# Rotary halves in chunks of their own, scores of 32 rows in fours, the norm's factor in the sine and cosine tables, and the short convolution's product from PSUM

## What is computed

```python
h = rmsnorm(x, mix_norm_g[l])
a_b, a_c, a_x, q, k, v, c_in = split(h @ w_in)            # 256,256,256,512,512,512,512 columns
y_a = a_b * causal_depthwise_conv(a_c * a_x, short_conv_w)  # 3 taps
q = apply_rope(q.reshape(b, s, 2, 4, 64), cos, sin)       # 2 maps x 4 heads of 64
k = apply_rope(k.reshape(b, s, 2, 4, 64), cos, sin)
# apply_rope: x1, x2 = halves of 32;  [x1*cos - x2*sin, x2*cos + x1*sin]
p = softmax(mask(q @ k.T / 8)); a = p[map 0] - lam * p[map 1]; y_b = rmsnorm(a @ v) * (1 - lam_init)
y_c = silu(layernorm(conv31(glu(c_in)) + bias))           # 31 taps: the "filter"
x = x + concat(y_a, y_b, y_c) @ w_out
```

## Time and profile before

| | |
|---|---|
| runs, us | 2670.54, 2681.98, 2677.64 |
| median, us | 2677.64 |
| profiled execution: time / span, us | 2680.19 / 2678.9 |
| mean granted TensorE clock | 0.983 |
| busy: PE, PEld | 2562.9 us (96%), 2112.5 us (79%) |
| busy: DVE, ACT, POOL | 1103.3 us (41%), 945.4 us (35%), 1211.0 us (45%) |

### The profile page before, as it was taken

How to read it: one execution, slowest core, us unless ns; L and a number is a source line. 1 busy time by engine, 2 the same in 40 slices (tenths; PEclk the granted TensorE clock), 3 DMA queues, 4 the chain that set the end, 5 groups by cost and what they waited for, 6 DMA issues and landing times.

```text
span 2678.9 us, 32969 instructions
## 1 busy us (share of the span) xinstructions
PE 2562.9 (96%) x12952; PEld 2112.5 (79%) x12952; DVE 1103.3 (41%) x2303; ACT 945.4 (35%) x1437; POOL 1211.0 (45%) x1597
## 2 busy tenths in 40 slices
PE   6999999999999999998999999999999999999998
PEld 5777888887777888886778788877777787888886
DVE  7965111126964211137656764423345523311112
ACT  4553322234453222244433233324453433322221
POOL 5114665653125656554332332344323554565653
PEclk8999999999999999999999999999998999999998
DMA  4442223225432222232110111122222231223222
GB/s 156 124 111 79 94 81 103 102 83 151 126 95 79 101 92 99 96 108 94 50 48 32 48 37 44 48 95 86 87 79 89 100 110 64 95 92 105 94 89 76
DMA packets 41371, 237.32 MB, mean 89 GB/s; under 512 B 4736, under 2 KB 5888, under 8 KB 18560
## 3 DMA queue, kind: packets, MB, share of 16 engines
q1 hardware_dynamic: 38912, 218.43, 23.4%
q0 software_dynamic: 2304, 16.78, 3.1%
HBM read 214.22 MB, written 4.19 MB: 82 GB/s over the span
## 4 chain that ended last, share of the span: by engine, by line
PE 84%; DVE 10%; ACT 3%; POOL 2%; issue 1%; DMA 0%; SPq 0%; DVEq 0%; ACTq 0%
PE PB L1757 67%; PE PB L1795 4%; PE PB L1759 4%; DVE cc L2413 2%; POOL WL L2788 2%; ACT WH L2016 1%; PE PB L1952 1%; PE PB L1971 1%; PE PB L1769 1%; PE PB L1777 1%; PE PB L1959 1%; PE PB L1919 1%; PE PB L1983 1%; PE PB L1999 1%; PE PB L1940 0%
## 5 line engine op out<-in xcount | busy, mean ns | idle before, releaser
L2788 POOL TENSOR_TENSOR WL<-WR,WH 128x256 fp32r<-128x256 f32 (+1 forms) x1444 | 1041.9, 757 | 789.1 <-ACT WH L2016 789.1
L1757 PE MATMUL PB<-HH,WH 128*128 128x512 f32 x1992 | 803.8, 404 | 12.2 <-ACT HH L2031 10.0
L1757 PE MATMUL PB<-HL,WH 128*128 128x512 f32 x1992 | 783.5, 393 | 1.9 <-DVE HL L2309 1.9
L1757 PE MATMUL PB<-HH,WL 128*128 128x512 f32 x1992 | 520.3, 397 | 2.6 <-POOL WL L2788 2.6
L2016 ACT ACTIVATE WH<-WR 128x2048 fp32r<-128x2048 f32 (+1 forms) x209 | 371.5, 1778 | 260.9 <-PE PB L1757 254.2
L1757 PEld LDWEIGHTS PB<-HH,WH 128*128 128x128 f32 x1992 | 378.4, 190 | 102.8 <-issue 14.3
L1757 PEld LDWEIGHTS PB<-HL,WH 128*128 128x128 f32 x1992 | 378.3, 190 | 80.0 <-issue 3.6
L1757 PEld LDWEIGHTS PB<-HH,WL 128*128 128x128 f32 x1992 | 366.0, 189 | 76.6 <-issue 3.9
L1757 PE MATMUL PB<-BL,WH 128*128 128x512 f32 x848 | 334.1, 394 | 0.8 <-DVE BL L2318 0.8
L1757 PE MATMUL PB<-BH,WH 128*128 128x512 f32 x784 | 310.6, 396 | 2.7 <-ACT BH L2045 2.7
L1757 PE MATMUL PB<-BH,WL 128*128 128x512 f32 x784 | 197.6, 396 | 5.4 <-POOL WL L2788 5.4
(11 more groups left out here) (344 smaller groups left out, 3103.1 us busy)
## 6 DMA issues: line engine op xcount, KB each, us to landing
WR<-in_w_gu SPq DMA_DIRECT2D x66, 1024.0 KB, 4.8
WR<-in_w_dn SPq DMA_DIRECT2D x48, 704.0 KB, 4.1
WR<-in_w_in SPq DMA_DIRECT2D x22, 1024.0 KB, 4.9
WL<-WR POOLq DMA_DIRECT2D x16, 1024.0 KB, 7.0
WR<-in_qkv SPq DMA_DIRECT2D x12, 1024.0 KB, 4.8
WR<-in_w_out SPq DMA_DIRECT2D x8, 1024.0 KB, 4.8
WR<-in_qk SPq DMA_DIRECT2D x8, 1024.0 KB, 4.8
WR<-in_gb SPq DMA_DIRECT2D x4, 1024.0 KB, 4.8
```

Of the source, the lines that this page charges most:

```text
L1757: ins = pe.matmul(out[:, 0:n], wt[:, k * cols + j * P:k * cols + (j + 1) * P], x[:, k, 0:n], start=first, stop=last)
L2788: ins = g.tensor_tensor(m.WL[u % 2][:, part], m.WR[u % 2][:, part], f32(m.WH[u % 2][:, part]), ALU.subtract)
```

## The change

- The weights of q and k are rearranged when the high part is cast: within a unit, the first halves (32 columns) of four heads come first, then their last halves. ScalarE does this in two instructions of 1024 elements, GpSimd reads the raw weights in the same order. So chunk p of `Q` and `K` holds first halves and chunk p + 2 last halves, and the rotation needs no swap of rows. These units (`of_heads`: 2, 3, 5 and 6) always have their low parts from GpSimd; `by_dma` now names units 4 and 7 to 10 in both layers. Before it named 4 to 10 in layer 0 and 2 to 10 in layer 1.
- `qkin` moves to ScalarE and only copies (q times 1/8). There are four buffers `qr`. `rotc` stays on GpSimd; VectorE multiplies `qr` by the sine in place (`rots`), and once both chunks of a pair are there, subtracts one and adds the other (`rot`). The matmul L1819 and its constant go.
- New tables `RCOS` and `RSIN`, `COS` and `SIN` times the norm's factor, are made once a layer on VectorE (`scaled`). The sign of the sine goes.
- `score` makes each product in two matmuls of 32 rows that add up in a bank: four heads' first halves side by side, then their last halves. It waits for all four banks first.
- `short_conv` multiplies the first tile by the square of the factor (`R2`, from ScalarE) and then by the second tile straight from PSUM: one VectorE operation less for each of its two halves.
- The model costs are new for these steps and for some that had none, and `FILTER_LEAD` is 1.0.

The core of the diff (the rest: constants' places, step and semaphore tables, model costs, the same steps' names):

```diff
@@ -137,15 +136,17 @@
     m.POSF, m.ANG, m.KF = run(tail1, end, ("POSF", [P, S]), ("ANG", [P, S]), ("KF", [P, S]))
+    qr2, qr3 = at("qr2", [P, S], b0 + 10 * S * 4)[0], at("qr3", [P, S], b1 + 10 * S * 4)[0]
     m.COS, m.SIN = run(g0, b0, ("COS", [P, S]), ("SIN", [P, S]))
...
     names = [("qr0", [P, S]), ("qr1", [P, S]), ("Q", [P, 4, S]), ("K", [P, 4, S]), ("VT", [P, 4, S]), ("cx", [P, 2 + S]),
-             ("cp0", [P, 30 + S]), ("cp1", [P, 30 + S]), ("cc0", [P, S]), ("cc1", [P, S]), ("ct", [P, S]), ("sm", [P, 96])]
+             ("cp0", [P, 30 + S]), ("cp1", [P, 30 + S]), ("cc0", [P, S]), ("cc1", [P, S]), ("ct", [P, S]), ("sm", [P, 96]), ("rcos", [P, S])]
     names += [(f"pa{i}{n}", [P, S]) for i in range(3) for n in range(2)]
-    m.qr0, m.qr1, m.Q, m.K, m.VT, m.cx, cp0, cp1, cc0, cc1, m.ct, m.sm, *pa = run(g1, b0, *names)
+    m.qr0, m.qr1, m.Q, m.K, m.VT, m.cx, cp0, cp1, cc0, cc1, m.ct, m.sm, rcos, *pa = run(g1, b0, *names)
     pa += run(tail1, end, ("pa30", [P, S]), ("pa31", [P, S]))
-    m.qr, m.cp, m.cc, m.cacc = (m.qr0, m.qr1), (cp0, cp1), (cc0, cc1), m.qr0
+    m.RCOS, m.RSIN, m.R2 = rcos, m.ct, rcos
+    m.qr, m.cp, m.cc, m.cacc = (m.qr0, m.qr1, qr2, qr3), (cp0, cp1), (cc0, cc1), m.qr0
     m.pa = [pa[2 * i:2 * i + 2] for i in range(4)]
@@ -305,8 +306,14 @@
+
+def of_heads(unit):
+    return unit[0] in ("w_in0", "w_in1") and unit[1] in (2, 3, 5, 6)
+
+
+
 def by_dma(unit):
-    return unit[0] in ("w_in0", "w_in1") and unit[1] >= (4 if unit[0] == "w_in0" else 2)
+    return unit[0] in ("w_in0", "w_in1") and unit[1] >= 4 and not of_heads(unit)
@@ -805,7 +812,7 @@
         w = f"w_in{l}"
-        qrs = Ring([Room(0), Room(1)], clock)
+        qrs = Ring([Room(i) for i in range(4)], clock)
         for q in qrs.rooms:
@@ -831,7 +838,8 @@
             step("rope_tab")
-            rope.extend([at("rt4"), at("rt5")])
+            rope.append(at("rt4"))
+        step("scaled", l, rope=rope, r=r, after=f + ct_after[0])
@@ -858,13 +866,14 @@
-        def rotate(name, c, q):
-            room = fbank.take()
-            t = Tile(room, room.after)
-            pe("rot", l, name, c, tile=t, q=q.i, tok=at("qkin", l, name, c), rope=rope, after=f)
-            room.free(at("rots", l, name, c))
-            q.free(at("rot", l, name, c))
-            turned[name, c] = True
+        def turn(name, c, q):
+            step("rots", l, name, c, q=q.i, tok=at("rotc", l, name, c))
+            turned[name, c] = q
+            if c >= 2:
+                first, second = turned[name, c - 2], q
+                step("rot", l, name, c - 2, first=first.i, second=second.i, tok=at("rots", l, name, c))
+                first.free(at("rot", l, name, c - 2))
+                second.free(at("rot", l, name, c - 2))
@@ -875,11 +884,12 @@
                     q = qrs.take()
-                    step("qkin", l, name, c, tile=t, q=q.i, r=r, after=q.after)
+                    step("qkin", l, name, c, tile=t, q=q.i, after=q.after + rope)
+                    step("rotc", l, name, c, q=q.i, tok=at("qkin", l, name, c), after=f)
                     room.free(at("qkin", l, name, c))
                     if waiting:
-                        rotate(*waiting)
-                    waiting = (name, c, q)
+                        turn(*waiting)
+                    waiting = name, c, q
                     yield
@@ -900,22 +910,22 @@
             it = chunks()
-            acc_after = [at("rot", l, "k", 1), at("rot", l, "k", 3)]
+            acc_after = [at("rot", l, "k", 1)]
+            step("r2", l, r=r, after=[at("rotc", l, "k", 1), at("rotc", l, "k", 3)])
             for j in range(2):
                 room, t = yield from tiles_of(it)
-                step("sh1", l, j, tile=t, r=r, after=f)
+                step("sh1", l, j, tile=t, after=f)
                 room.free(at("sh1", l, j))
...
                 room, t = yield from tiles_of(it)
-                step("sh2", l, j, tile=t, after=ct_after[0])
-                room.free(at("sh2a", l, j))
+                step("sh2", l, j, tile=t)
+                room.free(at("sh2", l, j))
                 yield
...
                 room, t = yield from tiles_of(it)
-                step("sh4", l, j, tile=t)
+                step("sh4", l, j, tile=t, after=acc_after)
                 room.free(at("sh4a", l, j))
-                ct_after[0] = [at("sh4", l, j)]
                 step("opv", "mix", l, j, src=m.cacc[:], c=j, tok=at("sh4", l, j), after=b_after)
@@ -1813,23 +1823,20 @@
             pe.matmul(PB[w["tile"].b][:], ones, m.cc[1][:], start=False, stop=True).then_inc(tile, 1)
-        elif kind == "rot":
-            te.all(w["tile"].after)
-            te.wait_ge(*at("qkin", *key))
-            pe.matmul(PB[w["tile"].b][:], m.CON[:, C_SWAP:C_SWAP + P], m.qr[w["q"]][:], start=True, stop=True).then_inc(tile, 1)
         elif kind == "score":
...
             n = P * (qb + 1)
-            for i in range(2):
-                c = 2 * i + pair
-                for k in range(2):
-                    te.all(w["tiles"][2 * i + k].after)
-                te.wait_ge(*at("rot", l, "q", c))
-                te.wait_ge(*at("rot", l, "k", c))
-                for k in range(2):
-                    rows = slice(64 * k, 64 * k + 64)
-                    pe.matmul(PB[w["tiles"][2 * i + k].b][:, 0:n], m.Q[rows, c, qb * P:(qb + 1) * P], m.K[rows, c, 0:n],
-                              start=True, stop=True).then_inc(tile, 1)
+            te.wait_ge(*at("rot", l, "q", pair))
+            te.wait_ge(*at("rot", l, "k", pair))
+            for t in w["tiles"]:
+                te.all(t.after)
+            for half, c in enumerate((pair, pair + 2)):
+                for u in range(4):
+                    rows = slice(32 * u, 32 * u + 32)
+                    ins = pe.matmul(PB[w["tiles"][u].b][:, 0:n], m.Q[rows, c, qb * P:(qb + 1) * P], m.K[rows, c, 0:n],
+                                    start=(half == 0), stop=(half == 1))
+                    if half:
+                        ins.then_inc(tile, 1)
         elif kind == "strans":
@@ -2013,7 +2020,13 @@
                 ae.wait_ge(*o.unit_end[u - 2].done)
-            a.activation(m.WH[u % 2][:, 0:n], m.WR[u % 2][:, 0:n], ACT.Copy).then_inc(sems["whi"], 1)
+            if of_heads(o.units[u]):
+                for j in range(2):
+                    ins = a.activation(m.WH[u % 2][:].rearrange("p (k j h x) -> p j k h x", j=2, h=4, x=32)[:, j],
+                                       m.WR[u % 2][:].rearrange("p (k h j x) -> p j k h x", j=2, h=4, x=32)[:, j], ACT.Copy)
+            else:
+                ins = a.activation(m.WH[u % 2][:, 0:n], m.WR[u % 2][:, 0:n], ACT.Copy)
+            ins.then_inc(sems["whi"], 1)
             if kind == "splitd":
@@ -2076,6 +2089,15 @@
             a.activation(m.cc[j][:], m.cc[j][:], ACT.Silu, bias=vec(f"ln_b{l}", j), scale=vec(f"ln_g{l}", j)).then_inc(sems["lnact"], 1)
+        elif kind == "qkin":
+            l, name, c = key
+            ae.wait_ge(*w["tile"].done)
+            ae.all(w["after"])
+            a.activation(m.qr[w["q"]][:], PB[w["tile"].b][:], ACT.Copy, scale=0.125 if name == "q" else 1.0).then_inc(sems["qkin"], 1)
+        elif kind == "r2":
+            ae.all(w["after"])
+            ae.wait_ge(*w["r"])
+            a.activation(m.R2[:], m.RSTD[:], ACT.Square).then_inc(sems["r2"], 1)
         elif kind == "vin":
@@ -2421,32 +2442,37 @@
             ins.then_inc(sems["lnmul"], 1)
-        elif kind == "qkin":
+        elif kind == "scaled":
+            l, = key
+            ve.all(w["rope"])
+            ve.all(w["after"])
+            ve.wait_ge(*w["r"])
+            v.tensor_tensor(m.RCOS[:], m.COS[:], m.RSTD[:], ALU.mult).then_inc(sems["rcos"], 1)
+            v.tensor_tensor(m.RSIN[:], m.SIN[:], m.RSTD[:], ALU.mult).then_inc(sems["rsin"], 1)
+        elif kind == "rots":
             l, name, c = key
-            ve.wait_ge(*w["tile"].done)
-            ve.all(w["after"])
-            v.scalar_tensor_tensor(m.qr[w["q"]][:], PB[w["tile"].b][:], 0.125 if name == "q" else 1.0, m.RSTD[:],
-                                   ALU.mult, ALU.mult).then_inc(sems["qkin"], 1)
+            q = m.qr[w["q"]]
+            ve.wait_ge(*at("rsin", l))
+            ve.wait_ge(*at("rotc", *key))
+            v.tensor_tensor(q[:], q[:], m.RSIN[:], ALU.mult).then_inc(sems["rots"], 1)
         elif kind == "rot":
-            l, name, c = key
-            q, dst = m.qr[w["q"]], (m.Q if name == "q" else m.K)
-            ve.wait_ge(*w["tile"].done)
-            ve.all(w["rope"])
-            ve.wait_ge(*at("rotc", *key))
-            v.tensor_tensor(q[:], PB[w["tile"].b][:], m.SIN[:], ALU.mult).then_inc(sems["rots"], 1)
-            ve.wait_ge(*at("rots", *key))
-            v.tensor_tensor(dst[:, c, :], dst[:, c, :], q[:], ALU.add).then_inc(sems["rot"], 1)
+            l, name, p = key
+            dst = m.Q if name == "q" else m.K
+            ve.wait_ge(*at("rots", l, name, p + 2))
```

(29 more changed lines are left out.)

18 lines of the change are left out of this document (8 added, 10 removed), and 4 rows, old and new, of the table ROUGH.

## The result

The changed kernel took 2686.1 us (median of 20 runs, 2679.6 to 2694.6) where the kernel before, on the same chip, took 2677.1: a ratio of 1.003 with a 95% interval of 1.0016 to 1.0044. The forecast was 2659.5 with a range of 2648 to 2677, so it was wrong by more than its range. The difference is within 0.5%, but it has the other sign.

What follows compares the result with a forecast made beforehand. TensorE was taken as the bound, VectorE next. Terms -13.9, -3.0, -5.5, -0.5, +1.3, +3.0 and +0.5 gave -18.1 us: 2680.2 to 2662.1 profiled, 2659.5 on the median's scale; range 2648 to 2677.

Steps and rivals of the forecast that it cites:

- Low parts moved from DMA to GpSimd: Six units' low parts on GpSimd slow VectorE's taps, up to 22 us; TensorE was charged 3 of 0 to 22.
- a room of 39 us: Layer 0: filter's high output ready at 159.0, output projection's first matmul at 198.1; taken as VectorE's slack.
- collisions: VectorE taps slowed beside GpSimd's six moved low parts: +3.0 us in the sum, own range 0 to 8.
- the long stall: TensorE's 10.45 us stand after projection unit 2 of layer 0; copies on ScalarE start unit 3 at 54.0: -5.5 us.
- the low part of unit 4: Layer 0: its DMA, issued later by GpSimd, lands about 70 to 73, wanted at 68 to 71: +1.3 us.
- the matmuls removed: 16 rotation matmuls, 8 per layer, leave TensorE's queue at 0.87 us each: -13.9 us.
- their waits: TensorE's waits at the rotations for scaled q or k and a bank, without the long one: -3.0 us.
- Scores in fours: Score matmuls of 32 rows, four side by side: cost as before, plus 0.5 us for more weight loads.
- rival 2: Only two row groups of score matmuls run at a time: 17.2 us more over both layers, 2676; chance 0.10.
- Rearranged casts: Casting high parts and reading raw weights in runs of 32: no extra taken, up to 0.2 us a unit on ScalarE.
- Rival 4: GpSimd too slow for TensorE, as reading in runs of 32 slows its pieces: +35 us, 2694; chance 0.05.
- Rival 3: VectorE replaces TensorE as bound: slowed taps delay masks and normalisations, and TensorE waits; put at 2671; chance 0.17.

Runs made afterwards that it cites:

- experiment 3: The kernel before, in its own order, with only the six low parts moved from DMA to GpSimd: 2692.6 us, ratio 1.0051.
- experiment 8: The kernel before with only the filter's lead changed from 2.0 to 1.0: 2674.2 us, ratio 0.9977.
- experiments 6 and 7: First: changed kernel with filter lead 4.0 instead of 1.0, 2688.7 us. Second: changed kernel with six low parts by DMA and lead 2.0, 2672.3 us.
- experiment 2: Changed kernel, order and waits untouched; GpSimd makes only 8 of each 256 columns of the six moved low parts: 2664.1 us, ratio 0.9928.
- experiment 1: Changed kernel with the six low parts by DMA again and halves set apart in the weights' memory layout: 2668.0 us, ratio 0.9952.
- 9: The changed kernel with six low parts by DMA, plus a seventh, unit 3 of layer 0: 2663.7 us, ratio 0.9951.
- 10: The changed kernel with seven low parts by DMA, plus an eighth, unit 2 of layer 0: 2662.8 us, ratio 0.9948.

## Why the prediction was wrong, point by point

The forecast was -18.1 us. The profile shows +4.6 at the start of the third stage, the median +9 with an interval of 4 to 12 by the ratio.

**Low parts moved from DMA to GpSimd: the step that failed.** The price for VectorE was right: six times 3.8, 22 us at most, and the taps grew by 18.5. Wrong was the share that TensorE pays. I took 3 of 0 to 22, and it paid 23.1, half clock included. The reason given was a room of 39 us, read from the filter's output in the earlier trace rows. That room was a property of the order of before. It says how early the taps were done, not how many microseconds VectorE has free: the same rows had VectorE at 95% in the weave. Every tap that takes 0.47 us more moves the mask, the row sum and the normalisation behind it, and TensorE's queue waits for them in order. The order of before has such a run too, nine taps ahead of its first mask (experiment 3), and laying GpSimd's 8.7 us over it would have shown a stall of some us. The Trainium skill, SBUF — State Buffer, section Who interferes with whom, named the mechanism, a VectorE instruction with two SBUF inputs against a GpSimd instruction that reads SBUF, and the trace agrees with it: the same eight taps take 1.14 us each beside full pieces and 0.67 beside short ones.

**The filter's lead was costed at nothing.** In the kernel before it is indeed no loss (experiment 8). In the changed order a lead of 1.0 goes with 6.7 us of waits for the filter and 10 us at half clock in layer 0; between unit 10 and the next layer the kernel of experiment 2 gives back 8.3 of its 15.1 us. I had read the filter's place in the old order and kept it, though the diff changed the number that sets it. But it isn't a loss that a longer lead wins back (experiments 6 and 7): with a lead of 2.0 and no wait of this kind for the filter, other waits give back 7.5 of 16.9 us in the same stretch. The lead decides what TensorE waits for there; what would save the time is open.

**The clock at the new stalls** had no term, since the new stalls had none: two stretches of 13.7 us. What they cost apart from the stalls was not measured.

**The rest of the sum held.** Experiment 2 is the change without collisions, for which the forecast was -18.1 - 3.0 = -21.1. It shows -18.5 at the third stage and -19.3 by the median's ratio. Within it, the long stall went better than forecast: in layer 0 unit 3 starts 8.7 us early, and half clock lasts 3 us there where before it was 13.7. In layer 0 the end of the weave was forecast 12 to 15 earlier and shows 15.1 (unit 10). Layer 1 was forecast 7 to 10 and gives 11.7. The stretch at the output projection of layer 0 took back the surplus. TensorE waits 0.7 us for the low part of unit 4 and 1.1 for that of unit 3, where 1.3 was charged. I didn't separate the matmuls removed from their waits, so these two terms are not shown one by one.

**Scores in fours.** The forecast holds and rival 2 falls. Groups of score matmuls of layer 0 in after, by shape; they answer to the earlier trace rows:

```profile
L1836 PE MATMUL PB<-K,Q 32*128 32x512 f32 x32 | 4.0, 613 | 0.0
L1836 PE MATMUL PB<-K,Q 32*128 32x256 f32 x32 | 3.2, 534 | 8.8 <-DVE sm L2500 8.8
L1836 PE MATMUL PB<-K,Q 32*128 32x384 f32 x32 | 3.1, 506 | 0.9 <-DVE sm L2500 0.9
L1836 PE MATMUL PB<-K,Q 32*128 32x128 f32 x32 | 1.5, 295 | 1.8 <-DVE K L2463 1.8
```

32 instructions of 512 columns take 4.0 us, where 16 took 4.3. Four run side by side: in the first blocks the four of a group start within 0.05 us. The 0.5 us for more weight loads isn't seen: 32 instructions of 128 columns take 1.5 us, where 16 took 1.6. The ideal by the row used in the forecast is 32 x 0.43 / 4 = 3.4. The Trainium skill, TensorE: Matmul & The Clock Gate, part 3, would give 32 x 0.43 / 3.07 = 4.5, an estimate from its factor; the row is below it.

**Rearranged casts.** No cost, as forecast: 8.62 us for a low part in runs of 32 beside taps, 8.74 for the plain one. Rival 4 falls. It was the only case well on the slower side, and it had the wrong mechanism.

**Rival 3** is what happened, with chance 0.17. Its top, 2678.5 with all 22 us passed on, was still too low by 8, for the stretch at the output projection and the clock weren't in it. The range was cut at 2677, below that top; a bound that the trace itself gives should have stood inside the range.

## What to carry to other kernels

When work moves to an engine that slows another, lay its stretches over the other's queue and ask who waits behind the slowed instructions; here, with the slowed engine 95% busy and a mask queued behind the taps, all of the slowing reached the bound. Ask the same of what stands behind the moved work in its new engine's queue (the cosine product in experiment 3). Slack read from a trace (an output that is early) belongs to that order: if the change touches the order or its parameters, it has to be read again. The rewriting itself is worth taking: rotation without TensorE, with the low parts left on DMA, is 0.5% faster than the kernel before (experiment 1, 9 and 10: 0.9952, 0.9951 and 0.9948), some 13 us.
